# RWKV: two buffers in turn for the second low-rank weights, fetched in the middle of the head pair before

## The reference, cut to what matters

```
w_log = -softplus(-(rw_w0[d] + tanh(wd) @ rw_w2[d])) - 0.5      # decay, per direction d
a     = sigmoid(rw_a0[d] + ad @ rw_a2[d])                       # in-context rate, per direction d
g     = sigmoid(gd) @ rw_g2                                     # output gate
out   = (norm(y) + bonus) * g
```

## Time and profile before

| what | us |
|---|---|
| runs of the kernel before | 4830.38, 4823.69, 4825.49 |
| their median | 4825.49 |
| the profiled execution's own time | 4828.52 |
| its span, first to last instruction | 4826.8 |

### The profile page before, as it was taken

How to read it: one execution, slowest core, us unless ns; L and a number is a source line. 1 busy time by engine, 2 the same in 40 slices (tenths; PEclk the granted TensorE clock), 3 DMA queues, 4 the chain that set the end, 5 groups by cost and what they waited for, 6 DMA issues and landing times. The chain is left out here.

```text
span 4826.8 us, 89082 instructions
## 1 busy us (share of the span) xinstructions
PE 4435.6 (92%) x40577; PEld 2797.0 (58%) x40577; DVE 1457.7 (30%) x2987; ACT 539.9 (11%) x1016; POOL 134.8 (3%) x253
## 2 busy tenths in 40 slices
PE   5899999999999999799999996999996999999995
PEld 2577868687767778577777774554443333333331
DVE  2133342425243333144445554111113111111112
ACT  1021211112112212000101000000011000000001
POOL 0000000000000000100000000000000000000000
PEclk7999999999999999899999996999997999999997
DMA  9111111111111110211111204886126999999997
GB/s 350 46 56 33 48 44 45 47 34 47 41 51 36 57 33 22 74 54 49 48 48 48 57 9 150 272 278 237 61 79 262 372 386 396 397 392 390 386 393 287
DMA packets 412691, 737.94 MB, mean 153 GB/s; under 512 B 16382, under 2 KB 255300, under 8 KB 389444
## 3 DMA queue, kind: packets, MB, share of 16 engines
q1 hardware_dynamic: 405060, 697.65, 40.2%
q0 software_dynamic: 7296, 35.13, 2.7%
HBM read 689.21 MB, written 43.52 MB: 152 GB/s over the span
## 5 line engine op out<-in xcount | busy, mean ns | idle before, releaser
L523 PE MATMUL psR<-hT,wrkv 128*128 128x320 f32 x3584 | 982.3, 435 | 16.4 <-DMA wrkv<-in_w_in 16.4
L523 PEld LDWEIGHTS psR<-hT,wrkv 128*128 128x128 f32 x3584 | 682.2, 191 | 300.7 <-DMA wrkv<-in_w_in 16.9
L1012 PE MATMUL psH<-hT,whg 128*128 128x320 f32 x2560 | 724.8, 439 | 26.1 <-DMA whg<-in_w_in 25.3
L1012 PEld LDWEIGHTS psH<-hT,whg 128*128 128x128 f32 x2560 | 484.5, 193 | 215.0 <-DMA whg<-in_w_in 25.8
L537 PE MATMUL psR<-X 64*64 64x64 f32 x8960 | 286.0, 219 | 7.9 <-ACT X L726 3.4
L1316 PE MATMUL psM<-branches,wmg 128*128 128x512 f32 x512 | 265.2, 600 | 23.4 <-DMA branches<-outr_scratch 23.1
L537 PEld LDWEIGHTS psR<-X 64*64 64x64 f32 x8960 | 272.0, 135 | 24.3 <-ACT X L726 9.4
L1490 PE MATMUL psO<-wout,mergedT 128*128 128x512 f32 x480 | 209.5, 599 | 5.9 <-DMA wout<-in_w_out 5.5
L833 DVE TENSOR_TENSOR X<-X,psR 128x256 f32<-128x256 f32 (+1 forms) x240 | 90.6, 377 | 382.2 <-PE psR L537 380.3
L1876 DVE SCALAR_TENSOR_TENSOR hid<-hid,psE 128x512 f32<-128x512 f32 x16 | 11.0, 687 | 586.7 <-ACT hid L1836 586.7
L1755 PE MATMUL psE<-hT,xg 128*32 128x512 f32 x1392 | 168.1, 601 | 3.8 <-DMA hT<-in_moe_w_up 3.2
(11 more groups left out here) (348 smaller groups left out, 4818.6 us busy)
## 6 DMA issues: line engine op xcount, KB each, us to landing
hT<-in_ada_w SPq DMA_DIRECT2D x64, 1024.0 KB, 8.7
wrkv<-in_w_in SPq DMA_DIRECT2D x56, 1024.0 KB, 5.9
mergedT<-in_moe_w_down SPq DMA_DIRECT2D x46, 1024.0 KB, 20.8
hT<-in_moe_w_gate SPq DMA_DIRECT2D x45, 1024.0 KB, 19.8
wmore<-in_moe_w_up SPq DMA_DIRECT2D x44, 1024.0 KB, 20.2
hT<-in_moe_w_down SPq DMA_DIRECT2D x43, 1024.0 KB, 21.7
hT<-in_moe_w_up SPq DMA_DIRECT2D x42, 1024.0 KB, 19.2
mergedT<-in_moe_w_up SPq DMA_DIRECT2D x42, 1024.0 KB, 19.9
```

The source lines that it names most:

```text
L523: mm = nc.tensor.matmul(ps[:, 2 * (n % 2) + h, 0:HALF], w[:, n % SLOTS, k, :], S["hT"][:, k, h * HALF:(h + 1) * HALF], start=(k == 0), sto ...
L1012: mm = nc.tensor.matmul(ps[:, 2 * (i % 2) + h, 0:HALF], w[:, i, k, :], S["hT"][:, k, h * HALF:(h + 1) * HALF], start=(k == 0), stop=(k == ...
```

## The change

`lw` gets a second buffer; pair r uses buffer r % 2, and each buffer has a semaphore of its own. The five transfers of pair r + 1 are issued behind weight tile n = 8 + 7r (the k tile of the next pair, sixth of the round's seven, index 5 when counted from 0) and no longer behind the third tile of round r + 1. From pair 2 on, SP waits ahead of them for the sums of pair r - 2, the last to use that buffer. GpSimd's zeroing covers both buffers. `s0` and `sout` become one buffer, and the load of a pair's start state waits for the store of the final state before it, where it waited for `s0_turned`.

```diff
-            nc.gpsimd.memset(S["lw"][:, :, :, :], 0.0).then_inc(s_z, 1)
+            nc.gpsimd.memset(S["lw"][:, :, :, :, :], 0.0).then_inc(s_z, 1)
...
-        s0, sout = sb("s0", [P, 2, L]), sb("sout", [P, 2, L])
+        s0 = sout = sb("s0", [P, 2, L])
...
-        g2, lora, ci = S["lw"], S["lora"], C["ci"]
+        g2, lora, ci = [S["lw"][:, i] for i in range(2)], S["lora"], C["ci"]
...
             def lora_weights(r):
-                if r:
-                    sp.wait_ge(sem("gate_sums"), r)
-                    sp.wait_ge(sem("lora_sums"), 2 * r)
+                if r >= 2:
+                    sp.wait_ge(sem("gate_sums"), r - 1)
+                    sp.wait_ge(sem("lora_sums"), 2 * r - 2)
                 for j, name in enumerate(("rw_w2", "rw_a2")):
                     for d in both:
-                        sp.dma_start(g2[L * d:L * d + L, j, d, :], I[name][0, d][:, r * P:(r + 1) * P]).then_inc(sem("lw_in"), 16)
-                sp.dma_start(g2[:, 2, 0, :], I["rw_g2"][0][:, r * P:(r + 1) * P]).then_inc(sem("lw_in"), 16)
+                        sp.dma_start(g2[r % 2][L * d:L * d + L, j, d, :], I[name][0, d][:, r * P:(r + 1) * P]).then_inc(sem(f"lw_in{r % 2}"), 16)
+                sp.dma_start(g2[r % 2][:, 2, 0, :], I["rw_g2"][0][:, r * P:(r + 1) * P]).then_inc(sem(f"lw_in{r % 2}"), 16)
...
-                if n >= 10 and (n - 10) % 7 == 2:
-                    lora_weights((n - 10) // 7 + 1)
+                if n >= 8 and (n - 8) % 7 == 0 and (n - 8) // 7 + 1 < PAIRS:
+                    lora_weights((n - 8) // 7 + 1)
...
-                    pool.wait_ge(sem("s0_turned"), 2 * r)
+                    pool.wait_ge(sem("final_out"), 32 * r)
...
-                W("lw_in", 80 * (r + 1))
+                W(f"lw_in{r % 2}", 80 * (r // 2 + 1))
...
-                    sums(g2[:, 0, d, :], lora[:, 0, :], 4)
-                    sums(g2[:, 1, d, :], lora[:, 1, :], 6).then_inc(sem("lora_sums"), 1)
+                    sums(g2[r % 2][:, 0, d, :], lora[:, 0, :], 4)
+                    sums(g2[r % 2][:, 1, d, :], lora[:, 1, :], 6).then_inc(sem("lora_sums"), 1)
...
-                sums(g2[:, 2, 0, :], lora[:, 2, :], 4).then_inc(sem("gate_sums"), 1)
+                sums(g2[r % 2][:, 2, 0, :], lora[:, 2, :], 4).then_inc(sem("gate_sums"), 1)
...
-... nc.sbuf_tensor("lw", [P, 3, 2, P], F32) as lw:
+... nc.sbuf_tensor("lw", [P, 2, 3, 2, P], F32) as lw:
```

More of the change, by code:

```diff
@@ L1995, in build_layer @@
             S["hT"] = hT
-            with nc.sbuf_tensor("lora", [P, 3, T], F32) as lora, nc.sbuf_tensor("lw", [P, 3, 2, P], F32) as lw:
+            with nc.sbuf_tensor("lora", [P, 3, T], F32) as lora, nc.sbuf_tensor("lw", [P, 2, 3, 2, P], F32) as lw:
                 S["lora"], S["lw"] = lora, lw
```

## The result

| what | before, us | after, us |
|---|---|---|
| median of the runs | 4826.59 (4823.69 to 4830.38, 4 runs) | 4758.94 (4755.44 to 4759.37, 4 runs) |
| profiled execution, own time | 4828.52 | 4758.85 |
| its span | 4826.8 | 4757.1 |

The ratio is 0.9858, 95% interval [0.9841, 0.9875]; the medians differ by 67.7 us, the profiled executions by 69.7. The forecast was 4757, with a gain of 68.3.

The account below looks back on a forecast made before the run. TensorE, busy in 92% of the span, was taken as the bound. Gain 68.96 less 0.7 for the table load gives 68.3; 4828.52 - 68.3 = 4760.2, against the median 4757 us, range 4748 to 4767.

Parts of the forecast that it names:

- Heads: RWKV rounds 1 to 7, third tile's issue to kk_sums: each falls to round 0's 10.58 us, gaining 68.96 us.
- The rival by which the clock returns its full half: Heads of rounds 1 to 7: by the page's formula 82 us come back, 4743 us; chance 0.01.
- the one by which only idle time comes back: Heads of rounds 1 to 7: something else lowers the clock, only 49.3 us return, 4776 us; chance 0.03.
- estimate by the penalty formula: Heads of rounds 1 to 7: idle time plus throttled time times share of pulses withheld, 73 to 86 us.
- The table load: ScalarE before `lorasum`, from round 1 on: its 1.28 us load may delay the second direction's sums, 0.7 us in all.
- The middle of the round: SP's queue behind the sixth tile: five issues take 4.42 us, 12.4 us are left on SP, cost zero.
- The slower rival: Mid-round transfers starve the weight tiles: slower from 9.8 us a round, 4841 us at 12 us a round; chance 0.02.
- SP's new waits: SP ahead of the transfers: waits for sums of pair r - 2 are already met, cost zero.
- GpSimd's new wait: GpSimd ahead of the `s0` loads: the `final_out` stores land 17.9 us before it is reached, cost zero.
- The memset: GpSimd's zeroing doubles from 0.74 to some 1.5 us beside L371's matmuls, cost zero; without that cover 0.7 us.
- Addresses, a semaphore more, later stages: Other SBUF addresses, one more semaphore to clear, last stage boundary shifting against the clock: taken as zero, 3 us either way.
- What was to be late next: In the head, VectorE still waits for TensorE before L775, 3.5 us instead of 12.76, not the other way round.

## Why the prediction was right

Point by point, by its own steps:

1. **Heads.** Round 0 as the model for all rounds: 10.58 us was forecast for each head, 10.57 or 10.58 came, for a gain of 69.01 against 68.96. The split into 49.3 us of idle time and 19.7 of slowed matmuls and restart stands: shorter stalls have both parts as well, by the table of stalls. The rival by which the clock returns its full half (4743) and the one by which only idle time comes back (4776) are both out. The prediction's estimate by the penalty formula of the Trainium skill ("TensorE: Matmul & The Clock Gate", "Terms") was 73 to 86 us in all; the measured 69.0 decides against it.
2. **The table load.** I allowed 0.7 us; it cost nothing that can be seen. The weight loads wait 1.3 us in seven heads for `lorasum`, the matmuls not at all. This term was mis-sized: measured 0.
3. **The middle of the round.** No idle time on `wrkv` beyond the first tile's 16.3 us, nor any with four times the transfers. The slower rival is out for the change as it is.
4. **SP's new waits.** The next tile is issued 17.23 us after the one before, as it was.
5. **GpSimd's new wait.** Nothing, in the change and by itself.
6. **The memset** took 1.38 us, estimated at 1.5, beside the matmuls of stage_lora.
7. **Addresses, a semaphore more, later stages.** 0.50 us behind kk_sums of round 7, within the 3 allowed. The parts from kk_sums to a round's end grew by 0.32 us in all, 0.05 a round; the prediction named any growth there as a sign against it and gave no size, but the mean of 201.22 us is still the 201.2 that it gave.

What was to be late next also came as worked out: VectorE stands 3.53 us before L775 in round 1, forecast at 3.5.

How near the number came is in part luck: the runs of one kernel lie 4 to 7 us apart, and the gain of 68.3 that was forecast stands between 67.7 by the medians and 69.7 by the profiled executions. What the traces confirm is the mechanism: 69.01 of the 69.67 us lie in the heads.

One thing the prediction did not have to know. It took the stall as a whole from the windows and did not ask which part of it was the issues and which the tile's transfer, and since the change takes all of the transfers out of the head, the gain does not hang on the answer. The runs show that both count: five transfers ahead of the tile leave 32.7 us of idle time, one single transfer behind it 42.1, one ahead of it 14.1. Nor does the gain need the second buffer: the change spends it because it puts the transfers in the middle of the round, where the first is still to be read.

## What to carry to other kernels

If one round of a loop happens to run without a stall, its windows are the forecast for the others, idle time, clock and all; then check that what follows lasts equally long in both kinds of round. A small transfer that is needed at once does not belong behind a large one on the same queue (here 2.0 us of idle time became 6.0). Before a second buffer is spent, look at when the last reader of the first one is done: here that was 12 us ahead of need, and one changed number gave the whole gain. Price a stall of TensorE by how much longer the whole stretch takes, slowed matmuls included, and not by its idle time alone (143.02 - 74.01 = 69.0 us here, of which 49.3 are idle).

## What was not expected of the hardware

- **One small transfer behind 1 MB is nearly as late as five.** With the one transfer of 64 KB behind the tile TensorE stood 6.0 us, with it ahead of the tile 2.0 us; with all five behind the tile it stood 7.2. The weight tiles themselves land 5.9 us after issue. The Trainium skill, page "DMA: Bandwidth & Descriptors", section "Queues, rings and completion order", says that descriptors of one issuing engine are taken in ring order on each DMA engine; the runs with the one transfer behind the tile and ahead of it agree with that.
- **A standstill of 2.0 us brought the clock down in three heads of seven** and left it in four, in one execution, with the same work ahead of it. What decides between them no run here shows.
- **With more traffic in the middle of a round TensorE had short waits that the trace gives no releaser for.** With four sets of transfers the next tile lands 6.9 us into the inverse (555.35 + 6.1 against a start at 554.56), in the changed kernel 2.6 us into it (550.63 + 5.7 against 553.76). A gap of 0.94 us then appears ahead of L541, put down to "issue", that is, to nothing that the profile shows; there are seven such waits, 3.5 us in all, where the changed kernel has one of 0.4. The part behind kk_sums grew to 202.31 us in round 1 and 201.90 in round 2, from 201.15 and 201.14. TensorE's timeline in round 1 of that kernel:

```profile
557.34 2.55 PE L541 MATMUL psR<-X 64*64 64x64 f32 x80 [0.23 <-ACT X L730]
560.12 1.78 PE L541 MATMUL psR<-X 64*64 64x64 f32 x53 [0.23 <-ACT X L730]
562.84 7.33 PE L541 MATMUL psR<-X 64*64 64x64 f32 x229 [0.94 <-issue]
```

The trace holds a candidate for what TensorE waited for. The view of the DMA queues has one called "instruction" (q8), on which a packet of 0.02 MB starts between 560 and 561 us here, as the tile's data end, nearly 6 us into the inverse; in the changed kernel the like packet starts between 556 and 557 us, 3 us into it. Here is the queue's row in these two windows, first of this kernel, then of the changed one:

```profile
q8 instruction: 1, 0.02, 7.8%
```

```profile
q8 instruction: 1, 0.02, 7.2%
```

That would be instructions held up behind the tile. But the trace does not say for which engine the packet was, and there was no run for it, so the cause stays open.
